# A list scheduler's step durations and one rule changed: the order in which three mixing blocks interleave with dense products on one Trainium2 core

## What is computed

```python
sc = jnp.einsum('bqhd,bsd->bqhs', iqb, ik32) * (IDX_DIM ** -0.5)
idx_score = jnp.einsum('bqhs,bqh->bqs', jax.nn.relu(sc), iwb)
_, sel = lax.top_k(idx_score, topk)
```

## Time and profile before

| what | value |
|---|---|
| median of three runs | 3038.27 us |
| the runs | 3038.21, 3038.27, 3054.9 us |
| the profiled execution, its own time | 3034.87 us |
| span of its instructions | 3033.1 us |
| mean granted TensorE clock | 0.993 |
| TensorE busy | 2962.9 us, 98% of the span |
| VectorE, ScalarE, GpSimd busy | 1583.6, 1077.8, 1408.2 us |
| moved by DMA | 248 MB, 82 GB/s |

### The profile page before, as it was taken

How to read it: one execution, slowest core, us unless ns; L and a number is a source line. 1 busy time by engine, 2 the same in 40 slices (tenths; PEclk the granted TensorE clock), 3 DMA queues, 4 the chain that set the end, 5 groups by cost and what they waited for, 6 DMA issues and landing times.

```text
span 3033.1 us, 42345 instructions
## 1 busy us (share of the span) xinstructions
PE 2962.9 (98%) x16912; PEld 2381.4 (79%) x16912; DVE 1583.6 (52%) x3162; ACT 1077.8 (36%) x1784; POOL 1408.2 (46%) x1805
## 2 busy tenths in 40 slices
PE   6999999999999999999999999999999999999999
PEld 5778887877888887767877778888877778888887
DVE  5776557565666316559744453333275773333310
ACT  4453334333222223323324432222354554332221
POOL 4554444335555554314333365555444334555553
PEclk9999999999999999999999999999999999999999
DMA  3211212112344422102112222223321112222232
GB/s 127 83 55 64 70 57 65 61 48 94 127 144 147 125 91 67 37 22 70 36 46 73 71 83 97 95 95 100 110 77 63 56 63 91 86 95 97 98 103 85
DMA packets 72069, 248.02 MB, mean 82 GB/s; under 512 B 8128, under 2 KB 8512, under 8 KB 71744
## 3 DMA queue, kind: packets, MB, share of 16 engines
q1 hardware_dynamic: 71872, 245.30, 25.0%
HBM read 243.18 MB, written 2.10 MB: 81 GB/s over the span
## 4 chain that ended last, share of the span: by engine, by line
PE 88%; DVE 9%; ACT 2%; issue 1%; POOL 0%; DMA 0%; SPq 0%; DVEq 0%; ACTq 0%
PE bank L1072 24%; PE bank L1074 24%; PE bank L1073 24%; PE bank L1106 3%; PE bank L1120 3%; PE bank L1569 1%; PE bank L1083 1%; PE bank L1587 1%; PE bank L1578 1%; DVE t L2211 1%; DVE sm L2209 1%; PE bank L1457 1%; PE bank L1112 0%; DVE t L1790 0%; PE bank L1490 0%
## 5 line engine op out<-in xcount | busy, mean ns | idle before, releaser
L2975 POOL TENSOR_TENSOR R<-W,R 128x256 fp32r<-128x256 f32 x1715 | 1301.4, 792 | 1510.0 <-ACT R L2573 1509.9
L1072 PE MATMUL bank<-u,R 128*128 128x512 f32 (+1 forms) x3440 | 1389.5, 404 | 13.3 <-DVE u L1746 3.2
L1074 PE MATMUL bank<-u,R 128*128 128x512 f32 (+1 forms) x3440 | 1347.4, 392 | 0.0
L1073 PE MATMUL bank<-u,R 128*128 128x512 f32 (+1 forms) x3440 | 1345.4, 391 | 0.0
L1072 PEld LDWEIGHTS bank<-u,R 128*128 128x128 f32 (+1 forms) x3440 | 648.1, 188 | 160.5 <-issue 11.0
L1074 PEld LDWEIGHTS bank<-u,R 128*128 128x128 f32 (+1 forms) x3440 | 646.9, 188 | 141.7 <-issue 0.8
L1073 PEld LDWEIGHTS bank<-u,R 128*128 128x128 f32 (+1 forms) x3440 | 648.8, 189 | 128.0 <-issue 5.0
L2573 ACT ACTIVATE R<-W 128x1024 fp32r<-128x1024 f32 (+2 forms) x452 | 451.3, 1005 | 140.1 <-PE bank L1074 132.7
L2603 ACT ACTIVATE u<-t 128x512 fp32r<-128x512 f32 x126 | 78.3, 630 | 305.7 <-DVE t L1768 249.6
L1779 DVE SCALAR_TENSOR_TENSOR X<-bank,X 128x512 f32<-128x512 f32 x32 | 22.1, 692 | 239.0 <-PE bank L1074 239.0
L1754 DVE TENSOR_TENSOR t<-bank,t 128x512 f32<-128x512 f32 x66 | 45.5, 689 | 174.4 <-PE bank L1074 164.5
(11 more groups left out here) (395 smaller groups left out, 2741.1 us busy)
## 6 DMA issues: line engine op xcount, KB each, us to landing
W<-in_in SPq DMA_DIRECT2D x48, 512.0 KB, 3.3
W<-in_ff_in SPq DMA_DIRECT2D x44, 512.0 KB, 3.3
W<-in_g_qkv SPq DMA_DIRECT2D x24, 512.0 KB, 3.3
W<-in_ada SPq DMA_DIRECT2D x24, 512.0 KB, 3.3
W<-in_f1g SPq DMA_DIRECT2D x22, 512.0 KB, 3.3
W<-in_f1u SPq DMA_DIRECT2D x22, 512.0 KB, 3.2
W<-in_f2g SPq DMA_DIRECT2D x22, 512.0 KB, 3.2
W<-in_f2u SPq DMA_DIRECT2D x22, 512.0 KB, 3.2
```

Source lines behind the costliest of these rows:

```text
L1072: e.matmul(b[0:cols, :], wh, hi, start=(k == 0), stop=False)
L1073: e.matmul(b[0:cols, :], wh, lo, start=False, stop=False)
L1074: i = e.matmul(b[0:cols, :], wl, hi, start=False, stop=(k == KT - 1))
L2975: i = e.tensor_tensor(R[q % NH][:, 1024 + a:1024 + b], W[p % NW][:, a:b], R[q % NH][:, a:b].bitcast(F32), SUB)
```

## The change

Two things change. The table `SEG` gets new durations for nearly all steps, and `weave` gets a constant `PATIENCE = 0.3`: a dense piece is taken only if the best chain step would become available more than 0.3 us after the moment at which the dense piece could start. The dense piece is priced at 1.40 in the new table (1.36 before), so 0.3 is about a fifth of it. No instruction is added, dropped or altered; the order in which each engine has them is another in the four woven stages. Line numbers behind line 310 rise by one.

```diff
-    dense="p1.36", sums="p.32 v2.0 s.69", xd="p.43 v.68", bt="p.43 s.6", cb="p.86 v.68", st0="v1.7", st="p.86 v1.14",
+    dense="p1.4", sums="p0.39 v3.4 s2.4", xd="p0.42 v0.65", bt="p0.42 s0.6", cb="p0.81 v0.65", st0="v2.12", st="p0.58 v1.19", ch="p0.27 v0.73",
...
-IN_SIGHT, FIRST = 12, 40.0
+IN_SIGHT, FIRST, PATIENCE = 12, 40.0, 0.3
...
-        if stream and stream[0] < offers.get("p", 1e9):
+        if stream and stream[0] + (PATIENCE if stream[1][0] == "dense" else 0.0) < offers.get("p", 1e9):
             offers["p"] = stream[0]
```

More of the change, by code:

```diff
@@ L293 @@
 SEG = {k: [[(x[0], float(x[1:])) for x in part.split("|")] for part in v.split()] for k, v in dict(
-    dense="p1.36", sums="p.32 v2.0 s.69", xd="p.43 v.68", bt="p.43 s.6", cb="p.86 v.68", st0="v1.7", st="p.86 v1.14",
-    ch="p.23 v.68", che="s2.1", cm="v.75|g1.3", sz="s.6 v.69", sy="p1.6 v1.6", sn1="s.63", sn1p="p.25", sn2="v2.7", sn2p="p.45", sn3="v.74",
-    pair="s.63 v.75", hq="p.86", hqs="s1.2", hn="v6.9", hnp="p.43", hn2="s.6", hg="p.23 v1.38 s1.23", hb="p.23 v1.5",
-    eq="p.43 s.6", ek="p.43 s.6", ea="v1.6", eb="v3.2", ec="v1.0", ep="p.43 s.6", hu="p1.72 v1.38", i0="g1.3|p.43 s.6 v1.5", il="p.55 s.6", ix="p.43 v.69", iu="p.43 s.6", ip="p.55 v.69", it="p.43 s.6", iq="g1.28", im="p.55 v.69",
@@ L298 @@
-    in_="p.55 v.65", hk="p.5 v2.0", hs1="p.22 v.35", hs2="p.22 s.28", hs3="p.54 v.33", ho="s.36", hon="v4.0",
-    hos="p.43", ho2="v.74", hz="s.6 v.69", conv="s.72 v2.24", conv2="s.63 v.75", gate="s.6", branch="v.7", part="v1.4", sh="s.69 v.74", wd="s.63",
-    ru="p1.2 s1.37", r1="v2.3 s.63", r1p="p.2", r2="v2.6", r2p="p1.72", r3="v2.3", r3p="p.86", r3b="v1.38", r4="v4.4|s1.9",
-    rm="p1.1 v1.38", rt="p.43 s.6", rz="g1.05", s1="p.43 s.27", s2="p.22 v.29", s4="p.43 v1.0", s3="p.54", ry1a="s.6",
@@ L302 @@
-    ry1="p.86 v.69", ry2a="s.62", ry2="p.2", ry2n="v2.6", ry3p="p1.72", ry3="v3.0", rg="s.63", ixp="s.6", ixw="p.05 v.2",
-    ixs="p.64 s.5 v.6", ixt="v1.2", ax="s.6", ap="s.6", av="p.43 s.6", an0="p.86", an1="s1.18", an2="v5.2", an2p="p.43",
-    an3="s.68", sa="p1.1 v1.37 s1.48", sb="v1.0", sc="p.27 s.43", sd="p.72", dg="s.6 v.69", do_="v.69", frq="p.86 v2.3", fr="p.86 v2.4",
-    ft1="s.6 v.45", ft1s="s.63", ft1p="p.86", ft2="v4.1", ft2r="s.63", ft3="v1.5", fc1="p.2", fc2="v3.6", fc3="p.45", fc4="v.74", gv="s.6", gu="s.6", gvt="p.43 s1.13",
@@ L306 @@
-    gn="v1.5 s.73", gnn="v5.7", gn2="v1.5", gs="p1.72 v1.5").items()}
+    dense="p1.4", sums="p0.39 v3.4 s2.4", xd="p0.42 v0.65", bt="p0.42 s0.6", cb="p0.81 v0.65", st0="v2.12", st="p0.58 v1.19", ch="p0.27 v0.73",
+    che="s1.68", cm="v1|g1.39", sz="s0.58 v0.65", sy="p1.84 v1.58", sn1="s0.62", sn1p="p0.85", sn2="v3.14", sn2p="p1.11", sn3="v0.67",
+    pair="s0.61 v0.77", hq="p0.86", hqs="s1.09", hn="v6", hnp="p0.38", hn2="s0.52", hg="p0.28 v1.58 s1.08", hb="p0.31 v1.37", eq="p0.41 s0.6",
+    ek="p0.35 s0.6", ea="v1.49", eb="v3.2", ec="v1.95", ep="p0.52 s0.49", hu="p1.74 v1.24", i0="g1.41|p0.48 s0.53 v1.58", il="p0.57 s0.58",
@@ new lines @@
+    ix="p0.48 v0.63", iu="p0.51 s0.59", ip="p0.56 v0.65", it="p0.53 s0.6", iq="g1.27", im="p0.55 v0.65", in_="p0.57 v0.59", hk="p0.53 v1.91",
+    hs1="p0.21 v0.34", hs2="p0.22 s0.27", hs3="p0.52 v0.22", ho="s0.35", hon="v4.82", hos="p0.44", ho2="v0.72", hz="s0.6 v0.62",
+    conv="s0.68 v2.27", conv2="s0.57 v0.77", gate="s0.61", branch="v0.92", part="v1.52", sh="s0.67 v0.72", wd="s0.63", ru="p1.06 s1.25",
+    r1="v2.83 s0.63", r1p="p0.83", r2="v3.51", r2p="p1.02", r3="v2.34", r3p="p0.88", r3b="v1.63", r4="v4.24|s1.67", rm="p1.02 v1.24",
@@ new lines @@
+    rt="p0.45 s0.54", rz="g0.99", s1="p0.58 s0.27", s2="p0.38 v0.29", s4="p0.6 v1.08", s3="p0.73", ry1a="s0.57", ry1="p0.68 v0.69", ry2a="s0.63",
+    ry2="p0.81", ry2n="v2.08", ry3p="p1.02", ry3="v3.42", rg="s0.58", ixp="s0.58", ixw="p0.34 v0.19", ixs="p0.87 s0.49 v0.61", ixt="v1.23",
+    ax="s0.6", ap="s0.59", av="p0.38 s0.51", an0="p0.86", an1="s1.07", an2="v5.63", an2p="p0.36", an3="s0.68", sa="p0.73 v1.35 s1.52", sb="v1.02",
+    sc="p0.26 s0.41", sd="p0.63", dg="s0.6 v0.59", do_="v0.66", frq="p0.74 v2.08", fr="p0.52 v2.24", ft1="s0.54 v0.48", ft1s="s0.52", ft1p="p0.84",
@@ L307 @@
+    ft2="v4", ft2r="s1.26", ft3="v1.58", fc1="p0.85", fc2="v2.8", fc3="p0.84", fc4="v0.75", gv="s0.9", gu="s1.89", gvt="p0.48 s0.67",
+    gn="v1.47 s0.67", gnn="v4.24", gn2="v1.96", gs="p1 v1.47").items()}
 EVACUATE = ("conv", "sz", "hz", "gate", "branch", "part", "sh", "ax", "ap", "dg", "gv", "gu", "ixp", "ixw", "ixs", "gvt", "gs")
```

## The result

The changed kernel takes 3053.34 us, the median of 19 runs (3051.5 to 3059.2); the kernel before takes 3039.24 us beside it, also of 19 (3036.98 to 3054.9). The ratio is 1.0045, with an interval of 1.0035 to 1.0054: slower by 14 us, where the forecast was 8 us faster and the range ended at 3051. The profiled execution of the changed kernel has a span of 3052.2 us, 19.1 longer than the 3033.1 of before; that one lies 4.4 us under the median of the 19. The kernel before has some four runs in five near 3039 us and the others near 3053, and since a ratio takes in all of them it can lie under the quotient of the medians.

The account below looks back on a forecast made before the run. TensorE, busy 98% of the time, was taken as the bound. Switches -10.4, patience +9.1, first stage -4, second -2.5, index scores 0, clock +1.5, other waits -1.5 gave -7.8 us: forecast 3030 us, range 3013 to 3051.

Parts of the forecast that it names:

- price of a held place: Mean real wait where the planner holds a dense piece back for a chain step: 0.07 us at each of 130 places.
- patience term: Waits at 130 held places in the four woven stages: 9.1 us more, range 0 to 25.
- patience costs more than it gives: Rival, chance 0.17: TensorE stands at the 130 places, a loss from 0.13 us each; at 0.25 us, 3054 us.
- Second stage: Gate pieces last to the stage's end, so half its 5.4 us of idle time goes: 2.5 us less.
- First stage: At its end, waits around the last state product and for a token sum mostly go: 4 us less, bounds 1 to 6.
- some 1.0 should stay: Of the 2.34 us TensorE waits for a token sum at the first stage's end, some 1.0 us remains.
- Index scores and clock: Third stage, row of 24 index scores: 24 to 25 us, change 0; falling clock there: 1.5 us more.
- the price of 11 us: Clock rival, chance 0.15: row of 24 index scores at 1.2 GHz and low clock behind it, 3040 us in all.
- Switches: TensorE goes from dense product to small step 55 times fewer, 0.19 us each: 10.4 us less.
- Hardly moves: Fourth stage: 75 instead of 76 switches and 13 held places; a move over 3 us would mean something missed.

Follow-up runs that it names:

- a1: The changed kernel with PATIENCE = 0, so only the new durations: 3051.4 us, ratio 1.0021 to the kernel before.
- b1: The kernel before with new durations and patience 0.3 in the first woven stage alone: 3039.07 us, ratio 1.0011.
- e3: The kernel before with a small step moved between two dense pieces at 36 places: 3038.95 us, ratio 1.0008.
- b2: The kernel before with new durations and patience 0.3 in the fourth woven stage alone: 3041.4 us, ratio 1.0017.
- c1: The kernel before with the planner's lag behind TensorE's share at 0.35 us instead of 0.2: 3051.72 us, ratio 1.0043.
- c2: New durations without patience, lag 0.35 us, in the last three stages; first stage as in the kernel before: 3070.27 us, ratio 1.0103.
- a4: The kernel before with new durations and patience 0.3 in the third woven stage alone: 3041.19 us, ratio 1.0001.
- b3: The changed kernel with PATIENCE = 0.15 instead of 0.3: 3045.6 us, ratio 1.001 to the kernel before.
- e1: The kernel before with the changed kernel's third stage and lag 0.35 us in the fourth: 3038.08 us, ratio 0.999.
- a3: The kernel before with new durations and patience 0.3 in the second woven stage alone: 3047.26 us, ratio 1.0027.

## Why the prediction was wrong, point by point

Two steps failed. One is the price of a held place, 0.07 us in the sum and 0.19 by the traces. The other is that the sum has no term for what new durations do to the order besides the gains it lists. Without its patience term it stood at -16.9 us; a1, the change without patience, has 414 changes from dense to small instead of 351, so that the same terms give -16.9 + 10.4 + 1.5 = -5 us for it, and it is slower by 12.5 us in the median, 6 by the ratio. That error of 11 to 17 us is there with no patience at all. What in the table's order costs it is known for some single waits only (below); the rest stays open.

**Patience: the first step that failed.** I took "a mean real wait of 0.07 us: 130 x 0.07 = 9.1 us more", because in the earlier trace rows VectorE starts 0.09 us ahead of the plan behind one `s2`. Measured are 24.7 us at these places. Even without the seven long ones it is 0.14 us a place, twice my value and about what the plan itself has there on average, 0.15. So the trace was not ahead of the plan where it mattered. One step of one stage, released by one engine, stood for all of them; the solve's steps that wait for ScalarE (L2702 above) were never looked at. And a step that is late costs more than the plan's 0.3 us, since nothing bounds it: the longest held places lose 2.2, 1.8 and 1.1 us. The term was too small by 15.6 us, of a total error of 22 to 23 (3053.3 against 3030). This says where the time is lost, not what leaving patience out would give: a1 leaves it out and is only 2 us faster by the median, 7 by the ratio. The sign that I had named for it, 15 us more idle time in the woven stages, did not come either: it rose from 34.7 to 44.9, since half of the loss stands in busy time. The rival "patience costs more than it gives" put its point of decision at 0.13 us a place and its time at 3054 us; 0.19 lies past that point and the time is 3053.3. It got there with 32.5 us for patience and -16.9 for the rest, both too large, and a1 shows that the rest, built by itself, is no gain. So its mechanism is seen at the held places, and its exact time is luck.

**Second stage: a gain that wasn't there.** I took 2.5 us of idle time away. It went from 7.5 to 12.8 us: waits over 0.3 us give 3.1 of the difference, shorter ones 2.2. The table alone (a1) has the long ones too, 9.6 us of them in 10.0 of idle time. My reading, which no run parted, is that chains in another order on TensorE meet VectorE's queue in another order. That a table could make long waits where there had been shorter ones was in none of my terms.

**First stage: half right.** The two waits went as said; one of 0.4 us for the same VectorE instruction now stands at an earlier state product. The wait for the cumulative sums, which I had said would stay at 3.5 us, is shorter:

```profile
PE bank L1156 <- DVE t L1834: 2.2, 1, 2.2
```

The step "some 1.0 should stay" of the token sum failed: 2.59 us are left and 10.2 us at the low clock follow. The stage is 4.0 us longer where I took 4 off. b1 however, this stage alone, has the time of the kernel before, and the old order of this stage took 217.7 to 221.7 us over ten traces; what is sure is that no gain came.

**Index scores and clock.** The row took 25.8 us, against 24 to 25 forecast and 25 before: right. The low clock lasted 27.3 us there, which by my own bound ("0.50 for more than 20 us") counts against me. What it cost seems smaller than that sounds. Behind the row the ten dense matmuls from 1374.74 to 1379.11 take 4.4 us instead of 2.3, so 2 us. Over the stage, work other than the scores lost some 3.6 us at the low clock, 0.8 before: 2.8 more, and 1.5 were taken. By the rule of the Trainium skill as I had applied it (TensorE: Matmul & The Clock Gate, "A second HAM failure mode: psum-queue depth-cycling") the row would run at 1.2 GHz for its whole length, which it does but for the first 2.7 us (the section speaks of a swing between the clocks, and here there was one fall); the price of 11 us that I had put on it did not come, and the row took 25.8 us where 25 were reckoned for before. That VectorE and ScalarE bound it, so that TensorE's clock costs little inside, is my reading; no run has the row at the full clock.

**Switches: open.** The term was -10.4 us. If each slot of TensorE is priced at the shortest tenth of its kind and neighbours over all the traces, the third stage has 7 to 10 us less of such work (33 changes fewer there), the second (22 fewer) and the fourth are within 1 us of before. One reason for the second may lie in the same slots: a transpose of the solve costs more ahead of another small step than ahead of a dense piece, 0.58 us against 0.36, so that bringing such steps together moves a cost as well as saving one. For the solve's steps of 16 matmuls it is the other way round, 0.47 ahead of a small step and 0.56 ahead of a dense piece. And the 0.09 that I had read for entering small steps compares two different groups of transposes (L1106 and L1160), so it was no clean price. The sign that I had named, a mean of the first matmuls of dense pieces below 404 ns, came and says little: L1073 has 403 where L1072 had 404, 2 us in all. e3 adds 36 changes and costs nothing that the time shows. Between those readings the term lies somewhere from 0 to -10 us. That it is not worth what waiting for it costs is settled by the sweep for the second stage, and for no other.

**Third stage.** It is 6.3 us longer, 4 to 6 against all the traces of the old order. The slots part this into 7 to 10 us less work, 9 more in waits, some 4 more around the scores and 3 at the low clock, an estimate that comes out at 6 to 9. Two waits of TensorE are new and long: the changed kernel has

```profile
PE bank L1098 <- DVE sm L1669: 3.8, 2, 2.1
```

for the norms of RWKV, whose VectorE part now stands behind rounds of the top-k. That the rounds delay it is read from the order and the times, no run parted them.

**Fourth stage.** "Hardly moves" stays just inside my own bound of 3 us: 2.8 in the changed trace, 2.7 in that of b2. One line's waits could make most of it; the row of before, then that of after:

```profile
PE bank L1578 <- DVE t L2388: 3.5, 7, 0.9
```

```profile
PE bank L1579 <- DVE t L2389: 6.7, 7, 2.3
```

Seven waits for the same VectorE instruction, 3.2 us more, one of them 2.3 us long. They come with the table: a1 has 7.7 us of them, without patience.

**The sum again**, in the windows of the two profiled executions, which are 20.9 us apart in the four stages: 24.7 us at held places; 4 around the scores and 3 at the low clock in the third stage; 1.5 in the first beside its held places; 5 less in other waits of the second, which has 6.8 more in all where its held places lose 11.9; and 7 to 10 less of work. That is 18 to 21 us. It is a list of where the time went, in which the terms are partly estimates; that it closes doesn't show that each is a cause.

## What to carry to other kernels

On an engine that is busy for 98% of the time, idle time bought on purpose is paid in full, and what it buys must be measured first: here 130 waits came to 0.19 us each, and in the second stage any patience over 0.15 us cost more than it gave. Build each half of a change by itself before blaming one: here each alone made the kernel slower, and the rule whose waits can be seen cost 17 to 20 us with the old durations and 2 to 7 with the new. Price a rule that adds many short waits with the mean over places of each kind, by each engine that releases them, and never by one sample; then measure from start to start, since the idle column showed half. A table of durations that is truer step by step need not give a better order: the second stage of before (454.5 us) was beaten by none of nine other orders tried (455.5 to 470.5), and with the lag as it was the new table alone made three of the four stages longer.

## What the hardware showed that I had not expected

**One order, two clocks.** In the trace of b2 the third stage has the order of the kernel before and the same idle time, 7.8 us, but is 597.1 us long instead of 580.7. The windows of that stretch, b2 and then before (columns as in the earlier trace rows):

```profile
1305.00:1314.00 9.00, 9.00 (x78) 6.96 (x78) 4.17 (x18) 1.52 (x4) 0.00 (x0) 1.00 0.01 2
1314.00:1351.50 37.50, 37.50 (x176) 25.74 (x175) 11.84 (x36) 7.81 (x19) 2.78 (x4) 0.50 0.03 8
```

```profile
1305.00:1314.00 9.00, 9.00 (x82) 6.94 (x81) 4.45 (x19) 1.52 (x4) 0.00 (x0) 1.00 0.01 2
1314.00:1351.50 37.50, 36.49 (x262) 26.11 (x260) 21.77 (x67) 13.31 (x28) 6.98 (x8) 1.00 0.08 29
```

In both, TensorE has no idle time ahead of 1314 us. In b2 the granted clock falls from 1.00 to 0.50 there, in the middle of RWKV's scan, and stays for 37.5 us; TensorE gets through 176 records in the time in which it does 262. The 16.4 us are about what lies between the runs of the kernel before (3037 to 3055), so I take this for their cause, though no trace of one of its long runs was at hand. The mean clock of its runs in the experiments fits: 0.985 to 0.988 in the 21 that took over 3048 us, 0.990 to 0.993 in the other 73. c1 and c2, where 19 and 16 scores are mixed with the scan, have such a fall too, of 34 and 48 us. Where the row of 24 index scores stands behind the scan (a4, b3, e1 and the changed kernel), none of the traces shows a long one in the scan, and none of the 22 runs of a4 and e1 lies above 3045 us, against 3 in 10 with the old order in b1, b2 and a3. That the mixed scores and scan steps cause it is my reading; no run tried it by itself.

**Repeatability.** At the full clock the second stage takes 454.4 to 454.6 us in six traces with the old order of that stage, and 462.30 and 462.33 in two with the new. A difference of 0.5 us in such a stage, without a fall of the clock, can be read from one trace, though whole runs spread over 15. The first stage, in which the clock falls at other places from run to run, spreads over 4 with one and the same order.
